# Two thirds of layer 1's modulation, loaded and consumed as single halves inside the last input projection

## The chip, the cores and the metric

The kernel runs on one core of a Trainium2 chip. The metric is the device time of one execution in microseconds (us). It was run three times: 2285.66, 2289.59 and 2289.63 us, median 2289.59 us.

## What is computed

The reference is a two-layer hybrid backbone on 256 latent and 256 context tokens of width 1024, all in float32. Cut to what the change touches:

```python
for i in range(DEPTH):
    sh1, sc1, g1, sh2, sc2, g2 = split(silu(c) @ mod_w[i] + mod_b[i], 6)      # and the same for c_ctx
    h  = modulate(rmsnorm(x, norm1_g[i]), sh1, sc1)
    hc = modulate(rmsnorm(xc, norm1_g[i]), sh1c, sc1c)
    m, mc = mixer(h, hc, ...)          # i == 1: conformer convolution | gated delta net
    x = x + g1 * m
    h = modulate(rmsnorm(x, norm2_g[i]), sh2, sc2)
    x = x + g2 * expert_choice_ffn(h, ...)
```

The modulation of a layer is a product of two vectors (latent and context conditioning) with a 1024 x 6144 matrix. The kernel computes it in three thirds of 2048 columns. Layer 1's first third (shift 1, scale 1) is needed before its mixer; the other two (gate 1, shift 2; scale 2, gate 2) are needed only after the mixer. Layer 1's mixer begins with the projection `h @ cd_w_in`, called cd here, whose 49 output tiles of 128 columns become q, k, v, output gates and the two halves of a gated linear unit.

## The kernel before, in words

**Weights and the ring.** All large weights pass through `ring`, three slots of 4 MB in SBUF. `weight_groups()` (line 56) writes out the order of the groups by hand; group n lies in slot n % 3. SyncE (SP) issues the loads in this order. Ahead of group n it waits until the counter `w_used` has reached n - 2, which says that the group three places earlier was consumed. TensorE (PE) waits for a group's landing (`group_in`, line 437) and raises `w_used` after the last matmul that reads the group.

The groups of this stage stand in the order cd0, cd1, third 1 half 0, third 1 half 1, cd2, cd3, third 2 half 0, third 2 half 1, cd4, cd5, cd6. A cd group holds eight tiles of the projection (the last one holds one). A half of a third is 512 of the 1024 input rows for all 2048 columns: 16 products per k-block and column group, accumulated in PSUM bank 6.

**The projection.** `project` (line 520 on) runs on PE over j = 0 to 50. In iteration j it first calls `between(j)`, here `cd_between` (line 480), then computes tile j into bank j % 4 (eight k-steps, line 538), then turns tile j - 2 if that is q, k or v (transposes at line 553 into banks 4 and 5). Tiles of q, og, ga and gb have 256 columns (latent tokens only), tiles of k and v and the tile "small" have 512. After "small", gb, ga the order repeats with a period of six: gb, ga, k, v, q, og, so tile 8 is og, 9 is gb, 10 is ga, 11 is k.

ScalarE (ACT) evacuates each tile (lines 1339, 1346, 1356) and applies silu to the tile before if it was convolved (line 1324); VectorE (DVE) runs the three-tap convolution of q, k and v (lines 1849 to 1853), copies the turned tile j - 2 (line 1857), multiplies the gated unit (line 1828), and fits the 31 taps of the conformer convolution (line 1815) into the iterations behind each ga tile. PE can be only a few tiles ahead: a tile needs its bank evacuated, a turn needs the silu and the copy of the turn two before.

**The modulation inside it.** `modulation_rows` (line 445) computes both halves of a third in a row, raises `w_used` after each, and raises `mod_rows`. ACT copies bank 6 to `mrow` (line 1262); PE turns `mrow` into bank 7 (`modulation_turn`, line 465, transposes at line 475); DVE adds the bias (line 1737). `CD_MODS = {2: 1, 4: 2}` places third 1 at j = 16 and third 2 at j = 32, each turned at j + 1 and added on DVE at j + 2.

**The gates of the delta net** share banks 6 and 7 with it. DVE forms the sums (iteration 20, `gate_cums`, line 1914), PE turns them at j = 28 (`gdn_gates`, line 714, matmuls at lines 718 and 719), DVE reads both banks in iteration 29 (lines 1879 to 1884) and raises `gate_gap`. PE waits for `gate_gap` before third 2 may write bank 6.

Of the kernel before, what the change touches and what calls it, by code (L numbers as in the profile page):

```python
# [49 lines left out]
CONF_STEPS = [(0, 7), (7, 13), (13, 19), (19, 25), (25, 31)]  # L50


CD_MODS = {2: 1, 4: 2}


def weight_groups():


    def mod(layer, r):
        return [(f"mod{layer}{r}", i, 1) for i in range(2)]  # L60

    g = mod(0, 0)
    g += [("gla", 8 * i, 1) for i in range(4)]
    g += mod(0, 1)
    g += [("ssd", 8 * i, 1) for i in range(3)]
    g += mod(0, 2)
    g += [("about", 4 * i, 1) for i in range(2)]
    g += mod(1, 0)
    g += [("moe0", i, 1) for i in range(12 * Q)]
    for i in range(7):  # L70
        if i in CD_MODS:
            g += mod(1, CD_MODS[i])
        g += [("cd", 8 * i, 1)]
    g += [("cdout", 4 * i, 1) for i in range(2)]
    g += [("moe1", i, 1) for i in range(12 * Q)]
    return g
# [22 lines left out]
def hybrid_backbone(nc, A, out):  # L99
    rg = Ring()  # L100
    with ExitStack() as ctx:
# [36 lines left out]
        def mod(layer, part, k, s):  # L138
            return modT[:, layer, 2 * part + k // 4, k % 4, s:s + 1]
# [133 lines left out]
        def sg(name):  # L273
            if name not in S:
                S[name] = sem(name)
            return S[name]
# [9 lines left out]
        def slot(n):  # L286
            return ring[:, n % RING, :, :]
# [146 lines left out]
        def _(pe):  # L434
            mm = nc.tensor.matmul

            def group_in(n):
                pe.wait_ge(landed[n % RING], rg.landed[n])
# [3 lines left out]
                for _ in range(n):  # L442
                    mm(ps[bank][:, 0:P], ident[:, :], ident[:, :], start=True, stop=True, skip_group_check=True)

            def modulation_rows(layer, r):

                first = rg.first[f"mod{layer}{r}"]
                if layer == 0 and r == 0:
                    pe.wait_ge(sg("cond_ready"), 1)
                else:  # L450
                    pe.wait_ge(sg("mod_row_copied"), 3 * layer + r)
                for kh in range(2):
                    if layer == 0 and r == 0 and kh == 1:
                        keep_warm(14, 0)
                    group_in(first + kh)
                    w = slot(first + kh).rearrange("p g (k n) -> p g k n", k=4)
                    for k in range(4):
                        for g in range(4):
                            last = mm(ps[6][32 * g:32 * g + 32, :], act_c[:, 4 * kh + k, :], w[:, g, k, :],
                                      start=(kh == 0 and k == 0), stop=(kh == 1 and k == 3),  # L460
                                      tile_position=(0, 32 * g))
                    last.then_inc(w_used, 1)
                pe.drain().then_inc(sg("mod_rows"), 1)

            def modulation_turn(layer, r):

                pe.wait_ge(sg("mod_row_copied"), 3 * layer + r + 1)
                if layer == 0 and r == 0:
                    pe.wait_ge(sg("norm_ms"), 1)
                else:  # L470
                    pe.wait_ge(sg("mod_added"), 3 * layer + r)
                    if r == 0:
                        pe.wait_ge(sg("norm_ms"), 2)
                for q in range(4):
                    nc.tensor.transpose(ps[7][:, q * P:(q + 1) * P], mrow[:, q * P:(q + 1) * P], ident[:, :])
                pe.drain().then_inc(sg("mod_turned"), 1)
# [4 lines left out]

            def cd_between(j):

                if j == 28:
                    gdn_gates()
                if j % 8 == 0 and j // 8 in CD_MODS:
                    if j > 28:
                        pe.wait_ge(sg("gate_gap"), 2)
                    modulation_rows(1, CD_MODS[j // 8])
                if j % 8 == 1 and j // 8 in CD_MODS:  # L490
                    modulation_turn(1, CD_MODS[j // 8])

            def norm(cw):

# [755 lines left out]
        def _(act):  # L1250
# [121 lines left out]
                    finish_conv(waiting)  # L1372
            def gate_softplus(j):

                if j % 8 == 7 and j // 8 + 1 in CD_MODS:
                    modulation(1, CD_MODS[j // 8 + 1])
                if j % 8 == 0 and j // 8 in CD_MODS:
                    act.wait_ge(sg("mod_turned"), 3 + CD_MODS[j // 8] + 1)
                if j == 30:
                    act.wait_ge(sg("gate_gap"), 2)  # L1380
                    A_(egl2, egl2, ACT.Exp)
                    A_(negc, gcT, ACT.Exp)
                    A_(ekd, ekd, ACT.Exp).then_inc(sg("gate_exps"), 1)
                if j == 42:
                    act.drain().then_inc(sg("kq_squared"), 1)
                if j == 44:
                    act.wait_ge(sg("root_in"), 4)
                    A_(rkq[:, 0:6, :], rkq[:, 0:6, :], ACT.Sqrt).then_inc(sg("root_out"), 1)
                if j == 1:
                    act.drain()  # L1390
                    A_(small[64:128, :], small[64:128, :], ACT.Sigmoid)
                if j == 3:
                    A_(small[64:128, :], small[64:128, :], ACT.Sqrt)
                if j == 6:
                    act.wait_ge(sg("sp_abs"), 2)
                    A_(alogx[0:64, :], cols[0:64, COL_AT["gdn_alog"]:COL_AT["gdn_alog"] + 1], ACT.Exp)
                    A_(g_u[0:64, :], g_u[0:64, :], ACT.Exp, scale=-1.0).then_inc(sg("sp_u"), 1)
                if j == 12:
                    act.wait_ge(sg("sp_w"), 2)
                    A_(g_l[0:64, :], g_w[0:64, :], ACT.Ln).then_inc(sg("sp_ln"), 1)  # L1400
# [329 lines left out]
        def _(dve):  # L1730
# [140 lines left out]
            def gate_softplus(j):  # L1871

                rows = slice(0, 64)
                if j % 8 == 2 and j // 8 in CD_MODS:
                    modulation(1, CD_MODS[j // 8])
                if j == 29:
                    dve.wait_ge(sg("gate_cums_turned"), 2)
                    tm = ps[7].rearrange("p (t d r) -> p t d r", t=NT, d=4)
                    V.tensor_copy(gcT, tm[:, :, 0:2, 0:8])
                    V.tensor_scalar(ngcT, tm[:, :, 0:2, 0:8], -1.0, None, ALU.mult)  # L1880
                    V.tensor_copy(sT, tm[:, :, 2:4, 0:8])
                    V.tensor_copy(egl2, ps[6][:, 0:256].rearrange("p (t d r) -> p t d r", t=NT, d=2)[:, :, :, 0:8])
                    dve.drain()
                    V.tensor_tensor(ekd, egl2, gcT, ALU.subtract).then_inc(sg("gate_gap"), 1)
                if j == 32:
                    dve.wait_ge(sg("gate_exps"), 2)
                    V.tensor_scalar(negc, negc, -1.0, None, ALU.mult)
                if j == 43:
                    key_sums(slice(0, 6), 1)
                if j == 45:  # L1890
                    key_scales(slice(0, 6), 4)
                    dve.drain().then_inc(sg("conf_ready"), 1)
                if j == 2:
                    dve.wait_ge(sg("proj_evacuated"), PLAN["cd"][0]["no"] + 1)
                    V.tensor_scalar(g_z[rows], small[rows, :], cols[rows, COL_AT["gdn_dtb"]:COL_AT["gdn_dtb"] + 1], None, ALU.add)
                    dve.drain()
                    V.scalar_tensor_tensor(g_u[rows], g_z[rows], -1.0, g_z[rows], ALU.mult, ALU.max).then_inc(sg("sp_abs"), 1)
                if j == 8:
                    softplus_head(rows, g_u, g_w, g_sp)
                if j == 14:  # L1900
                    softplus_end(rows, g_z, g_u, g_l, g_sp)
                    V.tensor_scalar(small[rows, :], g_sp[rows], alogx[rows, :], -1.0, ALU.mult, ALU.mult)
                if j == 16:
                    dve.drain()
                    V.tensor_tensor_scan(gcb[0:32, :], rst128[0:32, :], small[0:32, :], 0.0, ALU.mult, ALU.add)
                    V.tensor_tensor_scan(gcb[32:64, ::-1], rst128[32:64, :], small[32:64, ::-1], 0.0, ALU.mult, ALU.add)
                if j == 20:
                    dve.wait_ge(sg("cd_consts"), 2)
                    V.memset(albuf2, 0.0)
                    dve.drain()  # L1910
                    for t in range(NT):
                        for d in range(2):
                            e = t * P + edge(d)
                            last = V.tensor_scalar(albuf2[0:64, t, 32 * d:32 * d + 32], ident[0:64, 32 * d:32 * d + 32], gcb[0:64, e:e + 1], None, ALU.mult)
                    last.then_inc(sg("gate_cums"), 1)
# [839 lines left out]
```

## Time and profile before

| | us |
|---|---|
| median of three runs | 2289.59 |
| lowest, highest | 2285.66, 2289.63 |
| span of the profiled execution | 2285.4 |
| of it, the cd projection on PE | about 281 (1198.7 to 1480) |
| PE busy over the span | 1956.9 (86%) |
| DVE busy, ACT busy over the span | 721.3 (32%), 505.1 (22%) |

The profile shows one execution, from its first to its last instruction. That execution has no time of its own beside the span; the span lies 0.3 us below the lowest of the three runs and 4.2 us below their median. Times in rows are microseconds from the start of the span. In a timeline, instructions of one kind that follow each other are merged in a row; a bracket gives the idle time of the engine ahead of it and what ended it. A matmul in float32 leaves two records, so a projection tile has 16 records and a third of the modulation 64.

### The profile page before, as it was taken

The page shows a single profiled execution, that of the slowest core. Times are in us where ns is not written, and L with a number is a line of the kernel's source. Part 1 is how long each engine was busy: PE and PEld are TensorE (multiplying, and loading weights), DVE is VectorE, ACT ScalarE, POOL GpSimd, SP SyncE. Part 2 cuts the span into 40 slices and gives each one's busy share as a digit, 9 for nine tenths or more (in the row PEclk, how much of TensorE's full clock was granted, in tenths as well). Part 3 has the DMA queues.
Part 4 walks back from the last instruction along what each step waited for, and adds up shares of the span by engine and source line. Part 5 has one row for each costly group of instructions (what it writes and reads, how often), then busy time and mean ns, then how long its engine had stood idle before and what let it go on. Part 6 is the DMA issues. An engine that isn't in the chain of part 4 may idle for free.

```text
span 2285.4 us, 30387 instructions
## 1 busy us (share of the span) xinstructions
PE 1956.9 (86%) x13094; PEld 1027.2 (45%) x13094; DVE 721.3 (32%) x1306; ACT 505.1 (22%) x1072; POOL 164.7 (7%) x208
## 2 busy tenths in 40 slices
PE   7999899999999989889888898989999965655655
PEld 3444644445445333333236565677787721211112
DVE  2221743255213001010026775657774300000001
ACT  2432411243003000000024233354442100000001
POOL 0000000020000000000013000044440000000000
PEclk9999999999999999999999999999999988878788
DMA  9112121240217999999991524300002599999996
GB/s 385 44 74 85 63 112 74 103 192 1 92 63 314 433 431 430 431 431 430 431 378 74 211 85 157 141 10 2 2 2 83 231 385 431 431 431 431 431 431 263
DMA packets 34934, 527.26 MB, mean 231 GB/s; under 512 B 2416, under 2 KB 3696, under 8 KB 18544
## 3 DMA queue, kind: packets, MB, share of 16 engines
q1 hardware_dynamic: 33184, 522.55, 54.3%
q10 hardware_dynamic: 1616, 2.76, 0.4%
q8 instruction: 103, 1.69, 0.3%
q14 instruction: 31, 0.25, 0.0%
HBM read 524.26 MB, written 1.05 MB: 230 GB/s over the span
## 4 chain that ended last, share of the span: by engine, by line
PE 46%; DMA 31%; DVE 8%; issue 6%; PEld 5%; ACT 2%; DVEq 1%; PEldq 1%; ACTq 0%; SPq 0%; POOL 0%
DMA ring<-in_moe_w 29%; PE bank L538 13%; PE bank L1121 10%; PE bank L1016 5%; PEld bank L538 4%; PE bank L977 2%; DVE ring L1977 2%; PE bank L763 2%; PE bank L740 2%; DMA ring<-in_mod_w 1%; DMA ring<-in_cd_w 1%; DVE x L2381 1%; DVE x L1815 1%; PE bank L688 1%; PE bank L506 1%
## 5 line engine op out<-in xcount | busy, mean ns | idle before, releaser
L538 PE MATMUL bank<-hT,ring 128*128 128x512 f32 (+1 forms) x1504 | 552.6, 525 | 20.6 <-DMA ring<-in_cd_w 11.5
L1121 PE MATMUL bank<-ring,xgs 128*32 128x512 f32 x3048 | 384.4, 658 | 141.7 <-DMA ring<-in_moe_w 140.3
L538 PEld LDWEIGHTS bank<-hT,ring 128*128 128x128 f32 x1504 | 285.7, 193 | 267.8 <-issue 234.2
L1121 PEld LDWEIGHTS bank<-ring,xgs 128*32 128x32 f32 x3048 | 107.8, 119 | 391.1 <-issue 302.3
L1121 PE MATMUL bank<-ring,hT 128*32 128x512 f32 x1488 | 198.5, 689 | 78.3 <-DMA ring<-in_moe_w 78.3
L2227 DVE SCALAR_TENSOR_TENSOR x<-bank,modT,x 128x256 f32<-128x256 f32 x96 | 42.4, 480 | 474.6 <-PE bank L1147 474.6
L1121 PEld LDWEIGHTS bank<-ring,hT 128*32 128x32 f32 x1488 | 56.0, 124 | 207.9 <-issue 164.5
L1815 DVE SCALAR_TENSOR_TENSOR x<-gluR,cols,x 128x256 f32<-128x256 f32 x240 | 116.0, 484 | 16.6 <-issue 0.9
L2216 DVE TENSOR_TENSOR hT<-mrow,bank 128x512 f32<-128x512 f32 x16 | 10.9, 684 | 180.5 <-PE bank L1121 180.5
L2216 DVE TENSOR_TENSOR hT<-small,bank 128x512 f32<-128x512 f32 x8 | 5.5, 687 | 179.1 <-PE bank L1121 179.1
L1548 ACT ACTIVATE xgs<-bank 128x512 f32<-128x512 f32 x24 | 14.3, 597 | 202.8 <-PE bank L1093 202.8
L2567 POOL TENSOR_TENSOR ring<-ring,pmask 128x512 f32<-128x512 f32 x40 | 50.8, 1271 | 79.2 <-DVE ring L1965 70.1
L1016 PE MATMUL bank<-zmix,ring 128*128 128x512 f32 x128 | 56.1, 592 | 0.0
L1016 PE MATMUL bank<-mixA,ring 128*128 128x512 f32 x128 | 55.9, 592 | 0.0
L1558 ACT ACTIVATE mrow<-bank 128x512 f32<-128x512 f32 x16 | 9.5, 595 | 200.1 <-PE bank L1121 200.1
L1093 PEld LDWEIGHTS bank<-pick,htok 128*128 128x128 f32 x384 | 44.5, 191 | 18.7 <-issue 17.5
L1574 ACT ACTIVATE pgate<-bank 128x512 f32<-128x512 f32 x24 | 13.5, 595 | 177.2 <-PE bank L1121 177.2
L1147 PE MATMUL bank<-gateT,pgate 128*128 128x256 f32 x192 | 50.6, 394 | 0.3
L1558 ACT ACTIVATE small<-bank 128x512 f32<-128x512 f32 x8 | 4.8, 598 | 206.4 <-PE bank L1121 206.4
L763 PE MATMUL bank<-ring 64*64 64x64 f32 x1280 | 46.7, 223 | 4.1 <-ACT ring L1418 3.5
L2550 POOL MEMSET gluR<- 128x3008 f32 x1 | 2.6, 2610 | 659.2 <-DVEq L2237 659.2
L1093 PE MATMUL bank<-pick,htok 128*128 128x128 f32 x384 | 48.7, 281 | 0.7 <-DVEq L2198 0.7
(490 smaller groups left out, 2382.5 us busy)
## 6 DMA issues: line engine op xcount, KB each, us to landing
ring<-in_moe_w SPq DMA_DIRECT2D x93, 4096.0 KB, 22.4
ring<-in_mod_w SPq DMA_DIRECT2D x12, 4096.0 KB, 14.0
ring<-in_cd_w SPq DMA_DIRECT2D x6, 4096.0 KB, 17.4
ring<-in_ab_w SPq DMA_DIRECT2D x4, 4096.0 KB, 21.8
ring<-in_ab_wo SPq DMA_DIRECT2D x2, 4096.0 KB, 15.0
ring<-in_cd_wo SPq DMA_DIRECT2D x2, 4096.0 KB, 13.7
early<-in_moe_w SPq DMA_DIRECT2D x2, 2048.0 KB, 24.2
ring<-in_moe_w SPq DMA_DIRECT2D x2, 2048.0 KB, 18.4
```

Of the source, the lines that this page charges most:

```text
L538: last = mm(ps[p["no"] % 4][:, p["c0"]:T], w[:, k, :], hT[:, k, p["c0"]:T], start=(k == 0), stop=(k == KD - 1))
L740: last = mm(U4[r, d ^ hf, t, :], S[r, d, t, r], H[r, d ^ hf, t, :], start=True, stop=True, skip_group_check=True, tile_position=(64 * hf, ...
L763: last = mm(P4[r, v, t, :], H[r, v, t, :], Rs[r, v, t, :], start=True, stop=True, skip_group_check=True, tile_position=(64 * hf, 64 * hf))
L977: last = mm(ps[c % 4][:, SEQ:T], w[:, k, :], conf[:, k, :] if k < 8 else og[:, k - 8, :], start=(k == 0), stop=(k == 15))
L1016: last = mm(ps[c % 4], w[:, k, :], (mixA if k < 8 else zmix)[:, k % 8, :], start=(k == 0), stop=(k == 15))
L1093: last = mm(ps[(4, 7)[b % 2]][:, k * P:(k + 1) * P], htok[:, 2 * s + tt, ch:ch + P], pick[:, s, tt, P * q:P * q + P], start=(tt == 0), sto ...
L1121: last = mm(ps[banks + s][32 * j:32 * j + 32, :], lhs[s][:, 4 * kh + k, 32 * j:32 * j + 32], piece(g, n, 4 * k + j), start=(kh == 0 and k ...
L1147: last = mm(ps[(4, 7)[dt % 2]][:, 256 * s:256 * s + 256], yex[s][:, dt * P:(dt + 1) * P], gateT[:, s, q, :], start=True, stop=True, skip_g ...
L1815: V.scalar_tensor_tensor(y, gluR[:, i, :, w:w + GW], col("conf_w", 8 * w + i), y, ALU.mult, ALU.add)
L1977: last = V.copy_predicated(to[r, :, :, :], mask[r, 0, :].unsqueeze(1).unsqueeze(1).broadcast_to([64, 2, NT, 64]), S)
L2227: last = V.scalar_tensor_tensor(x[:, dt, cc], ps[(4, 7)[dt % 2]][:, cc], mod(layer, 5, dt, s), x[:, dt, cc], ALU.mult, ALU.add)
L2567: G.tensor_tensor(Hb[(l + 1) % 3], Fb[p % 2], pmask[:, l - 1, :].unsqueeze(1).unsqueeze(1).broadcast_to([P, 2, NT, 64]), ALU.mult).then_in ...
```

## The change

The four halves of the last two thirds stand singly in the ring's order: cd0, (1,0), cd1, (1,1), cd2, (2,0), cd3, (2,1), cd4, cd5, cd6, where (r, kh) is half kh of third r. Each is consumed alone, at j = 9, 18, 28 and 32. Third 1 is therefore turned at j = 19 and added on DVE in iteration 20; third 2 is turned at j = 33 as before. PE turns the gates of the delta net at j = 24 and DVE reads them in iteration 25; the wait for `gate_gap` stands ahead of half (2,0), at j = 28.

```diff
-CD_MODS = {2: 1, 4: 2}
+CD_HALVES = {9: (1, 0), 18: (1, 1), 28: (2, 0), 32: (2, 1)}
...
+    halves = mod(1, 1) + mod(1, 2)
     for i in range(7):
-        if i in CD_MODS:
-            g += mod(1, CD_MODS[i])
-        g += [("cd", 8 * i, 1)]
+        g += [("cd", 8 * i, 1)] + halves[i:i + 1]
...
-            def modulation_rows(layer, r):
+            def modulation_rows(layer, r, halves=(0, 1)):
...
-                for kh in range(2):
+                for kh in halves:
...
-                    group_in(first + kh)
+                    n = rg.at[f"mod{layer}{r}", kh]
+                    group_in(n)
...
-                pe.drain().then_inc(sg("mod_rows"), 1)
+                if halves[-1] == 1:
+                    pe.drain().then_inc(sg("mod_rows"), 1)
...
             def cd_between(j):
-                if j == 28:
+                if j == 24:
                     gdn_gates()
-                if j % 8 == 0 and j // 8 in CD_MODS:
-                    if j > 28:
+                if j in CD_HALVES:
+                    r, kh = CD_HALVES[j]
+                    if (r, kh) == (2, 0):
                         pe.wait_ge(sg("gate_gap"), 2)
-                    modulation_rows(1, CD_MODS[j // 8])
-                if j % 8 == 1 and j // 8 in CD_MODS:
-                    modulation_turn(1, CD_MODS[j // 8])
+                    modulation_rows(1, r, (kh,))
+                if j - 1 in CD_HALVES and CD_HALVES[j - 1][1] == 1:
+                    modulation_turn(1, CD_HALVES[j - 1][0])
...
 (ACT, gate_softplus)
-                if j % 8 == 7 and j // 8 + 1 in CD_MODS:
-                    modulation(1, CD_MODS[j // 8 + 1])
-                if j % 8 == 0 and j // 8 in CD_MODS:
-                    act.wait_ge(sg("mod_turned"), 3 + CD_MODS[j // 8] + 1)
+                if j + 1 in CD_HALVES and CD_HALVES[j + 1][1] == 1:
+                    modulation(1, CD_HALVES[j + 1][0])
+                if j in CD_HALVES and CD_HALVES[j][1] == 1:
+                    act.wait_ge(sg("mod_turned"), 3 + CD_HALVES[j][0] + 1)
...
 (DVE, gate_softplus)
-                if j % 8 == 2 and j // 8 in CD_MODS:
-                    modulation(1, CD_MODS[j // 8])
-                if j == 29:
+                if j - 2 in CD_HALVES and CD_HALVES[j - 2][1] == 1:
+                    modulation(1, CD_HALVES[j - 2][0])
+                if j == 25:
                     dve.wait_ge(sg("gate_cums_turned"), 2)
```

## Rows read from the trace of the kernel before

**Rows 1.** The page: span, busy time of TensorE, and granted clock in 40 slices.
```profile
span 2285.4 us, 30387 instructions
...
PE 1956.9 (86%) x13094; PEld 1027.2 (45%) x13094; DVE 721.3 (32%) x1306; ACT 505.1 (22%) x1072; POOL 164.7 (7%) x208
...
PEclk9999999999999999999999999999999988878788
```

**Rows 2.** Windows: start:end, length, busy PE, PEld, DVE, ACT, POOL, clock, DMA.
```profile
1198.00:1480.00 282.00, 261.35 (x1005) 165.71 (x1006) 193.40 (x393) 94.84 (x207) 23.30 (x71) 0.96 0.32 127
...
1297.00:1303.00 6.00, 5.71 (x20) 4.65 (x20) 0.00 (x0) 0.31 (x1) 0.00 (x0) 0.70 1.03 414
1303.00:1380.00 77.00, 76.40 (x271) 48.58 (x270) 60.50 (x128) 24.38 (x57) 0.00 (x0) 1.00 0.31 127
```

**Rows 3.** Timeline of TensorE in the cd projection: start, duration, instructions, idle before.
```profile
1244.43 0.66 PE L553 MATMUL bank<-ident,wk 128*128 128x128 f32 x4 [1.83 <-ACTq L1326]
1244.92 3.62 PE L538 MATMUL bank<-hT,ring 128*128 128x256 f32 x16
1252.97 0.66 PE L553 MATMUL bank<-ident,wk 128*128 128x128 f32 x2 [4.43 <-DVE k_t L1857]
1253.43 22.22 PE L538 MATMUL bank<-hT,ring 128*128 128x256 f32 x64
...
1284.43 7.07 PE L459 MATMUL bank<-ring,act_c 128*32 128x512 f32 x64
1297.29 5.36 PE L538 MATMUL bank<-hT,ring 128*128 128x256 f32 x16 [5.79 <-DMA ring<-in_cd_w]
...
1339.21 10.56 PE L538 MATMUL bank<-hT,ring 128*128 128x512 f32 x32 [0.26 <-issue]
...
1357.61 0.60 PE L718 MATMUL bank<-ident,small 128*128 128x128 f32 x4
...
1358.48 20.80 PE L538 MATMUL bank<-hT,ring 128*128 128x256 f32 x64
...
1380.10 7.07 PE L459 MATMUL bank<-ring,act_c 128*32 128x512 f32 x64
1392.91 5.34 PE L538 MATMUL bank<-hT,ring 128*128 128x256 f32 x16 [5.74 <-DMA ring<-in_cd_w]
```

**Rows 4.** The chain that ended last, around the two waits: start, duration, what.
```profile
1283.91 13.34 DMA ring<-in_cd_w
...
1379.36 13.51 DMA ring<-in_cd_w
```

**Rows 5.** Loads by tensor, cd weights and then modulation weights: issue to landing.
```profile
DMA to landing us min/median/max: 13.3/17.1/19.3
...
DMA to landing us min/median/max: 12.3/14.0/28.8
```

**Rows 6.** Timeline of VectorE in the cd projection, same columns.
```profile
1252.14 0.68 DVE L1857 COPY k_t<-bank 128x512 f32<-128x512 f32 x1
...
1281.89 0.48 DVE L1853 SCALAR_TENSOR_TENSOR wk<-wk,cols 128x256 f32<-128x256 f32 x1
...
1292.19 0.41 DVE L1857 COPY q_t<-bank 128x256 f32<-128x256 f32 x1
1303.23 0.43 DVE L1828 TENSOR_TENSOR gluR<-rstd,rst 128x256 f32<-128x256 f32 x1 [10.63 <-ACTq L1349]
...
1333.51 1.26 DVE L1914 TENSOR_SCALAR gts<-ident,small 64x32 f32<-64x32 f32 x8
...
1347.11 0.49 DVE L1849 TENSOR_SCALAR wk<-wk,cols 128x512 f32<-128x512 f32 x1 [2.04 <-ACTq L1341]
...
1357.95 0.69 DVE L1857 COPY v_t<-bank 128x512 f32<-128x512 f32 x1
...
1375.15 0.23 DVE L1879 COPY gts<-bank 128x64 f32<-128x64 f32 x1
...
1375.85 0.23 DVE L1884 TENSOR_TENSOR gts<-gts 128x64 f32<-128x64 f32 x1
```

More of the change, by code:

```diff
@@ L443, in keep_warm @@
                     mm(ps[bank][:, 0:P], ident[:, :], ident[:, :], start=True, stop=True, skip_group_check=True)
-            def modulation_rows(layer, r):
-                first = rg.first[f"mod{layer}{r}"]
+            def modulation_rows(layer, r, halves=(0, 1)):
                 if layer == 0 and r == 0:
@@ L451, in modulation_rows @@
                     pe.wait_ge(sg("mod_row_copied"), 3 * layer + r)
-                for kh in range(2):
+                for kh in halves:
                     if layer == 0 and r == 0 and kh == 1:
                         keep_warm(14, 0)
-                    group_in(first + kh)
-                    w = slot(first + kh).rearrange("p g (k n) -> p g k n", k=4)
+                    n = rg.at[f"mod{layer}{r}", kh]
+                    group_in(n)
+                    w = slot(n).rearrange("p g (k n) -> p g k n", k=4)
                     for k in range(4):
```

## The prediction

> **What bounds the kernel now.** I read the page first: TensorE (PE) is busy 86% of a span of 2285.4 us and its granted clock is at nine tenths or more until the last fifth [rows 1]. An average says nothing of one stage, so the windows come next. The cd projection takes 282 us, PE is busy 261.4 of them, VectorE (DVE) 193.4, ScalarE 94.8 [rows 2]. PE is the bound there, with some 20 us idle. The timeline of PE says where. Two gaps stand out, 5.79 and 5.74 us, both ended by a load of cd weights, both right behind the 64 records of a modulation third, and the tile behind each takes 5.36 and 5.34 us where a like tile takes 3.62 [rows 3]. A third gap of 4.43 us, at 1252.97, is ended by DVE [rows 3]. The chain of waits has the two loads in it, 13.34 and 13.51 us long [rows 4].
>
> Why the loads are late follows from the ring. While PE consumes cd1, the other two slots hold the two halves of the third. cd2 can be issued only when cd1 is consumed, at 1283.91 [rows 4], and must be there when the third is done, 7.07 us later [rows 3]. It took 13.3. The same happens at cd4.
>
> **The change, part by part.** No instruction is added or removed on PE, ScalarE, DVE or SP; they move.
>
> The two waits for cd2 and cd4 go, if the loads land in time under the new order. cd2's slot is that of half (1,0), consumed at j = 9, some 35 us before cd2 is needed at j = 16. cd3's slot is that of (1,1), consumed at j = 18; from there to tile 24 lie tiles 18 to 23 with their turns and the gates. That is two long tiles and four short ones, as long as tiles 28 to 31 [20.80, rows 3] plus two short tiles (6.9), about 29 us with turns. cd4's slot is that of (2,0), at j = 28; it is needed after tiles 28 to 31 and half (2,1), 20.8 + 0.8 + 3.5 = 25.1 us. The halves have longer still: (1,0) is loaded before the projection starts, (1,1) when cd0 is consumed (nine tiles ahead of its use), (2,0) when cd1 is (twelve tiles ahead), (2,1) when cd2 is (eight tiles ahead). Against this a cd load takes 13.3 to 19.3 us and a modulation load 12.3 to 28.8 [rows 5]. The tightest is cd4: 5.8 us to spare at 19.3, 3.7 us late at 28.8. I take it as in time. SP's order is safe too: consumption follows the load order, so no load sits behind one that waits for something later. Gain: 5.79 + 5.74 = 11.53 us.
>
> The slow tiles. The windows show a granted clock of 0.70 over the 6 us behind the wait and 1.00 in the 77 us after [rows 2]: PE fell to its 1.2 GHz level in the gap and came back to 2.4. Without the gap the tile takes 3.62 us: gain 1.74 + 1.72 = 3.46 us. Bounds: 0 if something else lowers the clock there, 3.46.
>
> Half (1,0) at j = 9. A half is half of 7.07, 3.54 us [rows 3], and in the old place it is wholly on the path. In the new one it stands between the turn that starts at 1244.43 and tile 9, so tile 9 ends near 1252.1 and not 1248.5. The turn behind it starts at 1252.97 in either case, because it waits for DVE's copy that starts at 1252.14 [rows 3, 6], and DVE's chain there does not touch the half. The 4.43 us gap shrinks to about 0.9 and the half costs nothing: gain 3.54 us. Were that cover gone, it would cost its 3.54 again.
>
> Tiles 10 to 13 follow that gap and take 22.22 us; the same mix (ga, k, v, q) takes 20.80 where no gap is ahead [rows 3]. With the gap at 0.9 I expect 20.8. But DVE is behind in this place: of the rows of its timeline between the copies at 1252.14 and 1292.19 none has more than 0.2 us of idle ahead of it (both ends in [rows 6]), and the turn of tile 13, just ahead of the third at 1284.43, needs the silu of a convolution that DVE ends at 1282.37 [rows 6]. So PE gets to the end of that turn about 1.0 us earlier, not 1.42. Bounds 0 and 1.42.
>
> DVE after j = 16. It idled 10.63 us for tile 16 [rows 6]. Now tile 16 is done near 1287 and DVE is free at 1292.6; it starts there, 10.6 us earlier than before, while PE is 8.5 us ahead of where it was less what half (1,1) costs at j = 18. DVE does not hold PE up: turns need convolutions two tiles old.
>
> The gates at j = 24. PE reaches them 5.79 + 1.74 + 1.0 + 3.54 = 12.1 us earlier than tile 24 started, at 1327.1. Their sums (ending 1334.8) come at least 10.6 us earlier, less 0.3 us for the bias that now precedes them, by 1324.5 [rows 6]. At least 2.6 us in hand, no wait.
>
> The wait for `gate_gap` at j = 28 is the new one. From the start of tile 24 PE needs 1357.61 - 1339.21 = 18.4 us to the end of the turn before tile 28 [rows 3]. DVE starts the convolution of tile 24 at 7.9 us after the same start (1347.11), has finished iteration 25's taps at 18.7 (1357.95), and reads the banks in 0.93 (1375.15 to 1376.08) [rows 6]: 19.7 us. PE waits 1.3 us, with half (2,0), tile 28 and the load of cd4 behind it; ScalarE and DVE then wait for tile 28. Cost 1.3 us. Bounds: 0, and 3 if DVE is two or so us later than in this walk. Before, four tiles lay between the two, so it cost nothing.
>
> Half (2,1) and the turns of both thirds stay on the path at their old price. Later stages only shift: the expert stage at the end starts its loads from a counter of the delta net, which shifts along.
>
> Sum: 11.53 + 3.46 + 3.54 + 1.0 - 1.3 = 18.2 us. The span would be 2267.2. The runs' median is 4.2 us above the profiled span, so the sum is taken off the median: 2271.4 us.
>
> A rule against it, weighed. Two rows show that a short wait alone does not slow the tile behind: after 1.83 us of idle the tile takes 3.62 us, the full-clock time [rows 3]. The Trainium skill, page "TensorE: Matmul & The Clock Gate", section "A second HAM failure mode: psum-queue depth-cycling", says that many small idles of PE between groups of matmuls can make the clock fall and rise again though none of them is long. By it the two long gaps would only be exchanged for clusters of short ones, and the sum would be some 14.7; by the row it is 18.2. The row is this kernel's own, so I take it and keep the other as a rival.
>
> **The rivals.** First, the clock falls at the short waits: the remaining 0.9 us at j = 9 and the 1.3 us at j = 28 each have low-activity matmuls of the modulation next to them, and the tile behind each costs 1.74 more. For it: the stretch behind the 4.43 us gap was 1.42 slow. Against: the 1.83 us row. Saving 18.2 - 3.5 = 14.7, time 2274.9.
>
> Second, only the waits go. DVE, whose lag the shortened gaps no longer let it make up, holds PE by some us at the turns of tiles 17 to 23, and takes what the half and the clock gave: saving 11.53 - 1.3 = 10.2, time 2279.4. For it: DVE works nearly without a break for 40 us up to 1292.6. Against: it has 282 - 193.4 = 88.6 us of idle in the stage [rows 2], and later it is idle ahead of convolutions, by 2.04 us at tile 24 [rows 6].
>
> Third, a load is late anyway, most likely cd4 behind (2,0): at 28.8 us the wait is 3.7 us plus a slow tile of 1.7. Saving about 13, time 2276.6.
>
> Fourth, the stage turns out bound by DVE and the end of the projection does not move by more than 4.6 us: time 2287.
>
> Fifth, slower: the three-step exchange of banks 6 and 7 (DVE's sums, PE's gates, DVE's read, PE's half) now has four tiles less on the first side and one tile less on the last. If DVE is late in it, PE stands at j = 24 and again at j = 28, and loads behind it are late as well. It decides the sign once these stalls exceed 18.2 us plus the threshold of 4.6, 23 us; the lag at the end of DVE's busiest stretch is 8.1 us (PE ends iteration 15 at 1284.5, DVE at 1292.6 [rows 3, 6]), so it would take three such on the path. At 23 us the time is 2294.4, and above it slower.
>
> **How the numbers follow.** Forecast 0.74, clock at short waits 0.10, only the waits 0.08, a late load 0.03, no effect 0.03, slower 0.02. About 0.2% (4.6 us) is what a measurement of this kernel can tell from no change. Faster 0.95, within 0.2% 0.03, slower 0.02. Low end: no new wait and the full 1.42 give 19.9 us; taken from a median that falls at the low run, 2285.7, it is 2265.8, rounded to 2265.5. High end: the first and third rival lie within 2277.0.
>
> **What would show it.** Right: no gap ended by a cd load inside the projection; 32 records of line 459 at four places, near 1245, 1294, 1348 and 1373, each 3.5 us; the gap at 1252.97 below 1.5 us; a gap of 1 to 2 us ended by line 1884 ahead of (2,0); the projection ending near 1462; a clock of 1.00 from 1300 to 1460. Wrong: PE gaps ended by DVE or ScalarE between tiles 16 and 24, tiles of 5.3 us after short gaps, or a gain inside the projection that is missing from the expert stage.

## The result and the profile after

The changed kernel takes 2270.94 us, median of four runs (2269.27 to 2272.80), against 2289.61 us for the kernel before beside it (four runs, 2285.66 to 2290.74). The ratio is 0.9923 with a 95% interval of 0.9911 to 0.9936, or 17.6 us less, between 15 and 20. The forecast was 2271.4 us.

The page of the changed kernel, its span, the granted clock, and the group of the projection's matmuls, whose last part is the idle time ahead of them and what ended most of it:

```profile
span 2267.6 us, 30389 instructions
...
PEclk9999999999999999999999999999999988878887
...
L539 PE MATMUL bank<-hT,ring 128*128 128x512 f32 (+1 forms) x1504 | 549.2, 523 | 9.2 <-ACT hT L1283 6.9
```

The same group on the page of the kernel before:

```profile
L538 PE MATMUL bank<-hT,ring 128*128 128x512 f32 (+1 forms) x1504 | 552.6, 525 | 20.6 <-DMA ring<-in_cd_w 11.5
```

The idle time ahead of the projection's matmuls fell by 11.4 us, and its largest part is no longer a load; of the 9.2 us left, 6.9 are the wait for h at the start of the stage. The matmuls themselves became 3.4 us shorter: same number, a better clock. Most line numbers are one higher after the change.

The timeline of TensorE (PE) in the cd projection after the change, to be laid beside [rows 3]. A half is 16 matmuls in all, so it leaves 32 records:

```profile
1245.12 0.66 PE L554 MATMUL bank<-ident,wk 128*128 128x128 f32 x4 [1.77 <-ACTq L1327]
1245.70 3.64 PE L458 MATMUL bank<-ring,act_c 128*32 128x512 f32 x32
1249.28 3.72 PE L539 MATMUL bank<-hT,ring 128*128 128x256 f32 x16
1253.66 0.41 PE L554 MATMUL bank<-ident,wk 128*128 128x128 f32 x2 [0.67 <-DVE k_t L1858]
1253.91 20.80 PE L539 MATMUL bank<-hT,ring 128*128 128x256 f32 x64
...
1278.97 0.65 PE L554 MATMUL bank<-ident,wk 128*128 128x128 f32 x4 [0.36 <-ACTq L1327]
...
1283.80 0.41 PE L554 MATMUL bank<-ident,wk 128*128 128x128 f32 x2 [0.72 <-DVE k_t L1858]
1284.04 10.49 PE L539 MATMUL bank<-hT,ring 128*128 128x256 f32 x32
1294.46 3.64 PE L458 MATMUL bank<-ring,act_c 128*32 128x512 f32 x32
1298.24 7.13 PE L539 MATMUL bank<-hT,ring 128*128 128x512 f32 x16
...
1347.19 0.38 PE L554 MATMUL bank<-ident,wk 128*128 128x128 f32 x2
1348.73 3.64 PE L458 MATMUL bank<-ring,act_c 128*32 128x512 f32 x32 [1.15 <-DVE gts L1885]
1352.30 20.91 PE L539 MATMUL bank<-hT,ring 128*128 128x256 f32 x64
...
1374.02 3.64 PE L458 MATMUL bank<-ring,act_c 128*32 128x512 f32 x32
1377.95 3.69 PE L539 MATMUL bank<-hT,ring 128*128 128x256 f32 x16 [0.29 <-issue]
```

Read it from the top. Half (1,0) stands at 1245.70, in front of tile 9, and the 4.43 us gap behind tile 9 has shrunk to 0.67. Tiles 10 to 13 take 20.80 us where they took 22.22. The other halves stand alone at 1294.46, 1348.73 and 1374.02, and no gap is ended by a load. The one new gap is the 1.15 us ahead of half (2,0), ended by VectorE's read of the banks.

The windows of the changed kernel say the same. Over the whole stage the mean clock rose from 0.96 [rows 2] to 0.99; what is left of the low clock lies in the first 5.5 us, behind the wait for h, and from there to the end of the projection it is 1.00, in the 8 us around the new gap too.

```profile
1198.00:1480.00 282.00, 272.08 (x1144) 173.13 (x1146) 201.26 (x404) 105.59 (x241) 26.91 (x74) 0.99 0.35 137
...
1344.00:1352.00 8.00, 6.85 (x50) 3.84 (x48) 7.11 (x19) 3.38 (x11) 0.00 (x0) 1.00 0.01 2
```

VectorE (DVE) after the change, to be laid beside [rows 6]: the multiplication of tile 16 at 1293.20 follows its predecessor without the 10.63 us of idle; the sums of the gates end at 1322.96; the banks are read from 1347.76 to 1348.68.

```profile
1292.87 0.41 DVE L1858 COPY q_t<-bank 128x256 f32<-128x256 f32 x1
1293.20 0.41 DVE L1829 TENSOR_TENSOR gluR<-rstd,rst 128x256 f32<-128x256 f32 x1
...
1321.70 1.26 DVE L1915 TENSOR_SCALAR gts<-ident,small 64x32 f32<-64x32 f32 x8
...
1336.91 0.49 DVE L1850 TENSOR_SCALAR wk<-wk,cols 128x512 f32<-128x512 f32 x1 [2.86 <-ACTq L1342]
...
1347.76 0.23 DVE L1880 COPY gts<-bank 128x64 f32<-128x64 f32 x1
...
1348.45 0.23 DVE L1885 TENSOR_TENSOR gts<-gts 128x64 f32<-128x64 f32 x1
```

**A yardstick for the experiments.** Single executions of one kernel differ by some us, for reasons that lie outside the edited part. So I measure each kernel's own trace from the start of tile 8 to the first matmul behind the projection that waits for the last copy. For the kernel before and the changed kernel these are the rows

```profile
1238.99 3.62 PE L538 MATMUL bank<-hT,ring 128*128 128x256 f32 x16
...
1480.96 1.98 PE L780 MATMUL bank<-small,ident 128*128 128x512 f32 x4 [0.66 <-DVE q_t L1857]
```

```profile
1239.72 3.62 PE L539 MATMUL bank<-hT,ring 128*128 128x256 f32 x16
...
1464.36 1.98 PE L781 MATMUL bank<-small,ident 128*128 128x512 f32 x4 [0.66 <-DVE q_t L1858]
```

that is 241.97 and 224.64 us, a saving of 17.33. The table has this stretch and the times of all kernels. The stretch is that of one execution of each kernel; the ratios come from four to ten executions. Each ratio is against the kernel before in the same set of runs, where its median was between 2288.53 and 2289.61 us, so ratios can be compared between rows and medians only roughly.

| kernel | stretch, us | against before | median, us | ratio (95% interval) |
|---|---|---|---|---|
| before | 241.97 | | 2289.61 | |
| changed | 224.64 | -17.33 | 2270.94 | 0.9923 (0.9911 to 0.9936) |
| third 1 alone | 229.93 | -12.04 | 2277.55 | 0.9954 (0.9939 to 0.9969) |
| third 2 alone | 236.63 | -5.34 | 2281.80 | 0.9973 (0.9963 to 0.9984) |
| half (1,0) at 10 | 230.12 | -11.85 | 2275.13 | 0.9945 (0.9930 to 0.9961) |
| half (2,0) at 29 | 223.43 | -18.54 | 2269.56 | 0.9915 (0.9898 to 0.9931) |
| half (1,0) at 15 | 240.39 | -1.58 | 2284.76 | 0.9979 (0.9970 to 0.9989) |
| before, 24 matmuls behind | 240.39 | -1.58 | 2286.14 | 0.9986 (0.9977 to 0.9996) |
| before, 12 matmuls behind | 245.00 | +3.03 | 2290.56 | 1.0004 (0.9995 to 1.0013) |
| before, 24 matmuls ahead | 240.33 | -1.64 | 2286.14 | 0.9984 (0.9974 to 0.9993) |

### The profile page after: what moved, and what is told of

The parts are those of the page before. It is cut to its first block, busy times and chain, and to the rows that moved or that the text cites. A ratio compares the mean times of both kernels' runs of the same rounds, so it can differ in the third digit from the quotient of the medians.

```text
span 2267.6 us, 30389 instructions
## 1 busy us (share of the span) xinstructions
PE 1955.6 (86%) x13094; PEld 1023.2 (45%) x13094; DVE 720.9 (32%) x1306; ACT 504.9 (22%) x1072; POOL 164.6 (7%) x208
## 4 chain that ended last, share of the span: by engine, by line
PE 50%; DMA 29%; DVE 9%; issue 5%; PEld 3%; ACT 2%; DVEq 1%; PEldq 0%; ACTq 0%; SPq 0%; POOL 0%
DMA ring<-in_moe_w 27%; PE bank L539 15%; PE bank L1122 11%; PE bank L1017 5%; PEld bank L539 3%; PE bank L978 2%; DVE ring L1978 2%; DVE x L1816 2%; PE bank L764 2%; PE bank L741 2%; DMA ring<-in_mod_w 1%; DVE x L2382 1%; PE bank L689 1%; PE bank L507 1%; PE bank L458 1%
## 5 line engine op out<-in xcount | busy, mean ns | idle before, releaser
L1575 ACT ACTIVATE pgate<-bank 128x512 f32<-128x512 f32 x24 | 13.5, 595 | 176.5 <-PE bank L1122 176.5
## 6 DMA issues: line engine op xcount, KB each, us to landing
ring<-in_mod_w SPq DMA_DIRECT2D x12, 4096.0 KB, 13.3
```

## The experiments

### The two thirds apart

Third 1 split, third 2 whole:

```diff
-CD_HALVES = {9: (1, 0), 18: (1, 1), 28: (2, 0), 32: (2, 1)}
+CD_HALVES = {9: (1, 0), 18: (1, 1), 32: (2, 1)}
...
-        g += [("cd", 8 * i, 1)] + halves[i:i + 1]
+        g += [("cd", 8 * i, 1)] + {0: halves[0:1], 1: halves[1:2], 3: halves[2:4]}.get(i, [])
...
-                if j == 24:
+                if j == 28:
                     gdn_gates()
...
-                    if (r, kh) == (2, 0):
+                    if r == 2:
                         pe.wait_ge(sg("gate_gap"), 2)
-                    modulation_rows(1, r, (kh,))
+                    modulation_rows(1, r, (0, 1) if r == 2 else (kh,))
...
-                if j == 25:
+                if j == 29:
                     dve.wait_ge(sg("gate_cums_turned"), 2)
```

> Only third 1 is split (halves at j = 9 and 18); third 2 stays whole at j = 32 and the gates at j = 28, as before. Theory (a late load, the slow tile behind it, and a half hidden under VectorE's lag): the wait for cd2 goes (5.79), the slow tile (1.74), half (1,0) is hidden (3.54), tiles 10 to 13 give 1.0: about 12 us below the kernel before, and the wait for cd4 of some 5.7 us with its slow tile stays. Rival (only the wait counts, VectorE takes the rest): about 6 us below.

Third 2 split, third 1 whole:

```diff
-CD_HALVES = {9: (1, 0), 18: (1, 1), 28: (2, 0), 32: (2, 1)}
+CD_HALVES = {16: (1, 1), 28: (2, 0), 32: (2, 1)}
...
-        g += [("cd", 8 * i, 1)] + halves[i:i + 1]
+        g += [("cd", 8 * i, 1)] + {1: halves[0:2], 2: halves[2:3], 3: halves[3:4]}.get(i, [])
...
-                    modulation_rows(1, r, (kh,))
+                    modulation_rows(1, r, (0, 1) if r == 1 else (kh,))
```

> Only third 2 is split (halves at j = 28 and 32, gates at j = 24); third 1 stays whole at j = 16. Theory: the wait for cd4 goes (5.74) and the slow tile (1.72), half (2,0) hides nowhere, a new wait of about 1.3 us for gate_gap comes ahead of it, and each half that stands alone costs 0.1 to 0.3 us: about 5.8 us below the kernel before, with the wait for cd2 left. Together with the run of third 1 alone it gives the whole change, about 17.8. Rival (the parts share one saving): the two savings do not add up to the whole.

The stretch became shorter by 12.04 us with third 1 alone and by 5.34 with third 2 alone. The sum, 17.38, is the 17.33 of the whole change: the two thirds save independently, and the rivals (6 us; one shared saving) are out. The times say the same less sharply: by the ratios 10.5 and 6.2 us, together 16.7 against 17.6. In each kernel the wait of the third that was left whole is still there. PE's timeline with third 1 alone:

```profile
1372.15 7.07 PE L458 MATMUL bank<-ring,act_c 128*32 128x512 f32 x64
1384.82 5.17 PE L539 MATMUL bank<-hT,ring 128*128 128x256 f32 x16 [5.59 <-DMA ring<-in_cd_w]
```

and with third 2 alone, where the new gap ahead of half (2,0) has the same 1.15 us as in the changed kernel although the stage runs 11 us later:

```profile
1297.45 5.58 PE L539 MATMUL bank<-hT,ring 128*128 128x256 f32 x16 [5.77 <-DMA ring<-in_cd_w]
...
1360.11 3.64 PE L458 MATMUL bank<-ring,act_c 128*32 128x512 f32 x32 [1.15 <-DVE gts L1885]
```

### Is half (1,0) hidden by VectorE's lag?

```diff
-CD_HALVES = {9: (1, 0), 18: (1, 1), 28: (2, 0), 32: (2, 1)}
+CD_HALVES = {10: (1, 0), 18: (1, 1), 28: (2, 0), 32: (2, 1)}
```

> The changed kernel with half (1,0) at j = 10 instead of 9, behind the turn that waits for VectorE. Theory: the half now stands behind the wait and not in it; the gap near 1253 is back at 4.3 us, the half costs its 3.5, the stretch behind the gap is 1.4 slow again, less the 1.1 us of short waits that TensorE then no longer has at tiles 14 and 15: 3.5 to 4.5 us above the changed kernel. Rival (the place of a half is worth nothing, the gain came from the loads alone): the same time as the changed kernel.

One tile later, the half is on the wrong side of the turn that waits for DVE:

```profile
1255.15 0.66 PE L554 MATMUL bank<-ident,wk 128*128 128x128 f32 x2 [4.43 <-DVE k_t L1858]
1255.74 5.78 PE L458 MATMUL bank<-ring,act_c 128*32 128x512 f32 x32
1261.46 20.91 PE L539 MATMUL bank<-hT,ring 128*128 128x256 f32 x64
```

The gap is back at 4.43 us to the digit. The stretch is 5.48 us longer than in the changed kernel (224.64 to 230.12); by the ratios the time is some 5 us longer, by the medians 4.2. So the place is worth what was claimed and more: I had expected 3.5 to 4.5, and in the stretch that range was missed by 1 us. What I had missed is who pays for the clock, and for how long. The windows of this run show it at its lower level (0.57 over 6 us) under the half, and back at 1.00 behind it:

```profile
1255.00:1261.00 6.00, 5.85 (x34) 1.58 (x34) 5.33 (x12) 3.04 (x10) 0.00 (x0) 0.57 0.00 0
1261.00:1283.00 22.00, 22.00 (x78) 12.99 (x71) 17.65 (x31) 5.42 (x10) 0.00 (x0) 1.00 0.50 192
```

The slowness falls on whatever stands behind the gap. For four tiles it cost 1.42 us, for the half 5.78 - 3.64 = 2.14. The two differ because the clock was low for a different time: from 1252.9 to 1256.3 us in the kernel before, from 1253.3 to 1260.1 here, by the profile's record of the clock. Whether the half itself kept it low for longer is not shown; one execution has it.

### The new wait for `gate_gap`

```diff
-CD_HALVES = {9: (1, 0), 18: (1, 1), 28: (2, 0), 32: (2, 1)}
+CD_HALVES = {9: (1, 0), 18: (1, 1), 29: (2, 0), 32: (2, 1)}
```

> The changed kernel with half (2,0) at j = 29 instead of 28. Theory: VectorE has read the banks 1.2 us into tile 28, so the wait for gate_gap goes and nothing takes its place: 1.2 us below the changed kernel, visible in the profile (no gap ended by line 1885) and hardly in the times. cd4's load has one tile less, about 21 us, and still lands. Rival: cd4 is now late and the gap comes back as a gap ended by the load.

```profile
1348.69 0.38 PE L554 MATMUL bank<-ident,wk 128*128 128x128 f32 x2
1348.91 3.62 PE L539 MATMUL bank<-hT,ring 128*128 128x256 f32 x16
1352.46 3.64 PE L458 MATMUL bank<-ring,act_c 128*32 128x512 f32 x32
```

The gap is gone, no other took its place, and the stretch is 223.43 us, 1.21 shorter than in the changed kernel. cd4 still lands in time with one tile less ahead of it. This is the shortest of all kernels here and it is well below the kernel before (0.9915). That it beats the changed kernel is shown by one trace of each; the medians, 2269.56 and 2270.94, were taken in different sets and could not tell 1.2 us.

### Is it the slot's release that makes a load late?

```diff
-CD_HALVES = {9: (1, 0), 18: (1, 1), 28: (2, 0), 32: (2, 1)}
+CD_HALVES = {15: (1, 0), 18: (1, 1), 28: (2, 0), 32: (2, 1)}
```

> The changed kernel with half (1,0) at j = 15 instead of 9, so that the slot of cd2 comes free only one tile ahead of its use. Theory (the slot's release times the load): cd2 is issued at the end of the half, lands 13.3 us later, and one tile and a turn (3.9 us) lie between: a gap of about 9.4 us ended by the load ahead of tile 16, a slow tile behind it (1.7), the half no longer hidden (3.5) and the slow stretch behind 1253 back (1.4), less some 1 us of waits for VectorE: 13 to 16 us above the changed kernel. Rival (loads are late because of the memory and not because of the slot): 3 to 5 us above.

PE's timeline and the chain of waits of this run:

```profile
1282.10 3.64 PE L458 MATMUL bank<-ring,act_c 128*32 128x512 f32 x32
...
1299.13 12.22 PE L539 MATMUL bank<-hT,ring 128*128 128x256 f32 x32 [9.07 <-DMA ring<-in_cd_w]
```

```profile
1285.80 13.28 DMA ring<-in_cd_w
```

A gap of 9.07 us, predicted 9.4, in a kernel whose halves all stand singly. The stretch is 15.75 us longer than in the changed kernel, inside the 13 to 16 expected; by the ratios the time is some 13 us longer, far from the 3 to 5 of the rival. So splitting the thirds is not what removes the wait. The wait is the load's 13.3 us less the work that stands between the release of the slot and the first use of what is loaded into it, and the place of the half sets that work.

### The slow tile behind the wait

Back in the kernel before, PE is kept busy while it would wait. Three versions: 24 matmuls of the identity behind each third, 12 behind it, 24 ahead of it.

```diff
                     modulation_rows(1, CD_MODS[j // 8])
+                    keep_warm(24, 7)
```

> The kernel before with 24 small matmuls of the identity (about 0.24 us each, 5.7 us) behind each of the two thirds, into bank 7, so that TensorE is busy while it would wait for cd2 and cd4. Theory (the slow tile is the clock, which falls in the gap): tiles 16 and 32 take 3.5 to 3.7 us instead of 5.36 and 5.34, the loads stay as late, and the time is 3.0 to 3.5 us below the kernel before. Rival (the tile is slow because the landing data or the ring hold it up): no change.

```diff
                     modulation_rows(1, CD_MODS[j // 8])
+                    keep_warm(12, 7)
```

> In the run kept warm with 24 small matmuls the loads of cd2 and cd4 took 14.5 and 14.2 us from issue, where five other such loads took 13.3 to 13.5. Theory (dense work of TensorE during the load holds the load up a little): 12 matmuls, half as long, hold it up half as much, landing 13.8 to 14.0; the gap is some 3.3 us, and the tile behind it may be slow or not. Rival (chance in the two loads): 13.3 to 13.5 again.

```diff
+                    keep_warm(24, 7)
                     modulation_rows(1, CD_MODS[j // 8])
```

> The kernel before with the 24 small matmuls ahead of each third instead of behind it. Theory (dense work during the load holds it up): the load again takes 14.1 to 14.5 us, since the same matmuls run in its window. Rival (only what runs at its end counts, or chance): 13.3 to 13.5. Either way the gap ahead of tiles 16 and 32 is below 1.5 us and these tiles take 3.5 to 3.8 us, because the modulation's own matmuls keep the clock up.

PE's timeline with 24 behind:

```profile
1291.25 5.62 PE L443 MATMUL bank<-ident 128*128 128x128 f32 x48
1298.06 3.72 PE L539 MATMUL bank<-hT,ring 128*128 128x256 f32 x16 [1.19 <-DMA ring<-in_cd_w]
```

with 12 behind, where a gap of 3.82 and later 3.47 us is left:

```profile
1301.31 5.19 PE L539 MATMUL bank<-hT,ring 128*128 128x256 f32 x16 [3.82 <-DMA ring<-in_cd_w]
...
1397.56 6.54 PE L539 MATMUL bank<-hT,ring 128*128 128x256 f32 x16 [3.47 <-DMA ring<-in_cd_w]
```

and with 24 ahead:

```profile
1286.32 5.52 PE L443 MATMUL bank<-ident 128*128 128x128 f32 x48
1291.78 7.07 PE L459 MATMUL bank<-ring,act_c 128*32 128x512 f32 x64
1300.29 3.72 PE L539 MATMUL bank<-hT,ring 128*128 128x256 f32 x16 [1.44 <-DMA ring<-in_cd_w]
```

With a gap of 1.2 or 1.4 us the tile takes 3.72 us, with its data just landed. So the slow tile is the clock and not the fresh data, as the theory had it: 5.36 - 3.72 = 1.64 us, and 1.62 at tile 32. With gaps of 3.8 and 3.5 us the tile takes 5.19 and 6.54: the clock falls in those too, and the second, shorter gap cost more. The windows of this version (12 matmuls) show how:

```profile
1299.00:1301.00 2.00, 0.00 (x0) 0.00 (x0) 0.00 (x0) 0.00 (x0) 0.00 (x0) 0.98 0.99 393
...
1301.00:1306.00 5.00, 4.69 (x15) 3.93 (x16) 0.00 (x0) 0.00 (x0) 0.00 (x0) 0.67 1.03 411
...
1397.00:1403.00 6.00, 5.44 (x13) 4.36 (x14) 0.00 (x0) 0.00 (x0) 0.00 (x0) 0.50 1.02 408
```

In the 3.82 us gap the clock was still full almost to its end and fell as the tile began, at 1300.9; it was back at 1304.3. In the 3.47 us gap it fell at 1396.5, 1.1 us before the tile began, and stayed low to 1403.3, for all but the last 0.8 us of the tile.

But the stretch became only 1.58 us shorter with 24 matmuls, not 3.0 to 3.5 (by the ratio 3.2 us, between 0.9 and 5.3, which can't tell the two apart). In the trace this expectation failed, because the loads took longer and gave 1.16 and 0.66 us of the gain back. The chain of waits has them at

```profile
1283.52 14.50 DMA ring<-in_cd_w
...
1378.48 14.16 DMA ring<-in_cd_w
```

against 13.34 and 13.51 in the kernel before [rows 4]. With 12 matmuls they took 14.45 and 14.31, with 24 ahead 14.36 and 14.07. All six loads of these kernels lie between 14.1 and 14.5 us, the five like loads of the other kernels (two before, one each in three versions) between 13.3 and 13.5. In all of them the next load is issued some 4 us behind, only with 24 ahead 10 us. Half the matmuls did not halve it, so neither expectation for the version with 12 holds; the one for 24 ahead does (14.1 to 14.5 again). That the matmuls are the cause is not shown: in the version with half (1,0) at 10, which has none, the load of cd2, issued at 1261.60 with no other under way, took 14.1 us too, and a modulation load of the kernel before, issued at 1339.03, took 14.1. The cause stays open. The version with 12 matmuls is a warning all the same: in its traced execution the stretch is 3 us longer than in the kernel before, of which 1.9 are the longer loads and 1.0 the clock, and in the times nothing was gained (ratio 1.0004, from 1.1 us less to 3.0 us more).

## Why the prediction was right

The sum was 18.2 us; the stretch shows 17.33, the span 17.8, the ratio 17.6 with an interval of 15 to 20, and the two medians differ by 18.7. The mechanism was right part by part. That the median came within 0.5 us of the forecast is in part luck: the sum was 0.9 too large in the stretch, and single runs of one kernel lie 5 us and more apart. Step by step:

**The two waits and the hidden half**, 11.53 + 3.54 = 15.07 us. A third and the wait behind it took 12.86 us from the first row of the third to the tile [rows 3: 1284.43 to 1297.29], and 12.81 at the second place. The three halves that now stand on the path take 3.78, 3.57 and 3.93 us from their start to the start of the next tile, 11.28 together. So 14.39 us went. The mechanism is shown by the runs with half (1,0) at 10 and at 15; the term was 0.7 too large, because a half that stands alone took up to 0.4 us more than half of a third. The prediction had put that at nothing.

**The slow tiles**, 3.46 us. Tile 16 is at full speed again (1.74), tile 32 takes 3.53 from start to end where it took 5.18 (1.65): 3.39. Shown to be the clock by the kernels kept warm.

**Tiles 10 to 13**, 1.0 us of a possible 1.42. From the start of tile 8 to the turn of tile 13 it was 45.11 us before (to 1284.10) and is 44.08 now (to 1283.80): 1.03. The missing 0.4 is the 0.72 us wait for DVE in front of that turn, as the walk had it.

**The new wait**, 1.3 us. The turn starts at 1347.19 and the half at 1348.73, 1.54 us later, of which about 0.2 is the turn; the profile puts 1.15 down as idle, and moving the half gave back 1.21. The walk through DVE's iterations 24 and 25 was right to a tenth, because nothing in it changed but the place where the banks are read.

14.39 + 3.39 + 1.03 - 1.3 = 17.5, and 17.33 was measured; the 0.2 between them is not traced.

**The loads.** The margins were larger than I had allowed. cd3, issued at 1298.16, landed after 12.9 us and was needed 31 us after its issue; cd4, issued at 1352.43, landed after 12.9 us and was needed after 25.5. The 19.3 and 28.8 us that I had held against them [rows 5] were the longest in the kernel before; in the new order cd3, cd4 and cd5 took 12.9, 12.9 and 13.3. The longest in the stage was cd2, 15.4 us, issued at 1249.41 while half (1,1), issued at 1239.08, was still landing; it was needed only 34.6 us after its issue.

**The gates at j = 24** did not wait: their sums ended at 1323.0 and PE reached them at 1328.2, 5 us in hand where the bound was 2.6.

**The rivals.** No clock loss at the short waits: after 0.67 us of idle four tiles take 20.80, behind the 1.15 us gap and its half 20.91, and the clock over that window is 1.00. So the rule of the Trainium skill that was weighed ("TensorE: Matmul & The Clock Gate", "A second HAM failure mode: psum-queue depth-cycling") did not show here, in a float32 kernel, with gaps of 0.3 to 1.8 us. DVE did not take the gain: no gap of PE between tiles 16 and 24 is ended by it, and it is back to waiting for ScalarE by tile 24 (2.86 us). The slower rival had 5 us in hand at its first step and 1.15 us of wait at its last; it was far from the 23 us that it needed.

Where the single runs spread: the first eight tiles, which the change does not touch, took 39.5 to 41.2 us from kernel to kernel, 39.59 before and 40.59 in the changed one, and the part from the projection to the end 804.4 and 803.2. With the 0.3 us by which the changed kernel was earlier at the start of the stage that is, and not the edited part, the difference between 17.33 and 17.8. The first eight tiles differ by the clock behind the wait for h: it was low until 1201.7 us before, until 1203.4 in the changed kernel, and 2 us more at half the clock are 1 us of work.

## What to carry to other kernels

In a ring of n slots filled in order, ask of each load what was consumed n places earlier, and how much work of the consumer lies between that and the first use; where two short items follow each other the work is too little, and spreading them between long ones removes the wait without another slot. When small work must go somewhere in the engine that sets the pace, put it just ahead of an instruction that waits for another engine anyway: one place later it cost 5.5 us and not nothing. And price a gap of the matmul engine together with the low clock of what stands behind it; half filling a gap gained nothing here.

## What was not expected

A load of cd weights with another close behind it took 14.1 to 14.5 us in all three kernels with added matmuls and 13.3 to 13.5 in the others, whether 12 or 24 were added, ahead or behind; but loads of 4 MB with nothing else under way took anything from 12.4 to 14.1 us in kernels without such matmuls, so this difference of 1 us is no proof of a cause.

And a gap of 3.47 us left TensorE slow for longer (6.54 us for the tile) than one of 3.82 us (5.19), where the original gaps of 5.79 and 5.74 cost 5.36 and 5.34: the loss behind a gap does not grow with the gap. The profile's record of the clock settles what it does follow. The loss is half of the time that TensorE works at the low clock:

| gap, us | clock low | of it, TensorE at work | half of that | measured loss |
|---|---|---|---|---|
| 5.79 (before) | 1293.8 to 1300.7 | 3.36 | 1.7 | 5.36 - 3.62 = 1.74 |
| 3.82 (12 matmuls) | 1300.9 to 1304.3 | 3.01 | 1.5 | 5.19 - 3.62 = 1.57 |
| 3.47 (12 matmuls) | 1396.5 to 1403.3 | 5.75 | 2.9 | 6.54 - 3.62 = 2.92 |
| 9.07 (half (1,0) at 15) | 1292.2 to 1302.5 | 3.34 | 1.7 | 12.22 - 10.49 = 1.73 |

A long gap can spend half of the low stretch or more while nothing runs; in a short one the fall comes late and the work behind it pays. What decides when the clock falls and how long it stays low is not shown by these runs.
